# Four pairs of conditioning units move from layer 0's FFN to the norm in the middle of layer 1

## The reference

```python
def adaln(c, w, b):
    return jnp.split(jax.nn.silu(c) @ w + b, 6, axis=-1)

def modulate(x, g, shift, scale):
    return rms_norm(x, g) * (1.0 + scale[:, None, :]) + shift[:, None, :]

for layer in range(DEPTH):
    mp = adaln(c_prompt, w_ada[layer], b_ada[layer])
    ms = adaln(c_sample, w_ada[layer], b_ada[layer])
    hp = modulate(yp, g_mix[layer], mp[0], mp[1])
    hs = modulate(ys, g_mix[layer], ms[0], ms[1])
    ...  # mixer: convolution and linear attention in layer 0, gating and window attention in layer 1
    yp = yp + mp[2][:, None, :] * (op @ w_out[layer])
    yp = swiglu_sublayer(yp, mp[3], mp[4], mp[5], g_ffn[layer], w_ffn_gate[layer],
                         w_ffn_up[layer], w_ffn_down[layer])
    ...  # the same for ys
```

## Time and profile before

| what | value |
|---|---|
| median of 3 runs | 2774.05 us (2773.72 to 2775.11) |
| the profiled execution | 2771.56 us, span 2769.8 us |
| PE busy | 2686.3 us, 97% of the span |
| DVE, ACT, POOL busy | 1427.0, 1161.6, 96.4 us |
| granted TensorE clock, mean | 0.986 |
| DMA | 603.61 MB, 218 GB/s over the span |

### The profile page before, as it was taken

One profiled execution on the slowest core, in us unless ns is written; L12 is line 12 of the kernel. 1 busy time (PEld: TensorE's weight loads), 2 busy tenths in 40 slices (PEclk: granted clock), 3 DMA queues, 4 the chain that ended last, 5 costly groups with the idle time before them and its releaser, 6 DMA issues.

```text
span 2769.8 us, 48514 instructions
## 1 busy us (share of the span) xinstructions
PE 2686.3 (97%) x20155; PEld 2479.4 (90%) x20155; DVE 1427.0 (52%) x1983; ACT 1161.6 (42%) x1521; POOL 96.4 (3%) x136
## 2 busy tenths in 40 slices
PE   5899999999999999999999999998999999999998
PEld 1688987889889888998999899898999999999998
DVE  0588957564444333444544556656554444444444
ACT  2433255454343322343443446535444433444433
POOL 1100011110000000000000000001000000000000
PEclk7999999999999999999999999999999999999999
DMA  9877769677777788777465454334545455455453
GB/s 399 360 288 273 289 234 167 266 273 277 284 272 283 273 315 329 281 277 264 154 233 163 143 184 138 101 124 164 165 165 167 140 167 181 164 167 167 137 164 127
DMA packets 110043, 603.61 MB, mean 218 GB/s; under 512 B 24830, under 2 KB 26302, under 8 KB 53579
## 3 DMA queue, kind: packets, MB, share of 16 engines
q1 hardware_dynamic: 109898, 601.56, 62.2%
HBM read 592.02 MB, written 9.49 MB: 217 GB/s over the span
## 4 chain that ended last, share of the span: by engine, by line
PE 89%; DMA 5%; DVE 3%; ACT 2%; issue 1%; SPq 0%; DVEq 0%; ACTq 0%
PE ps L880 26%; PE ps L882 25%; PE ps L881 25%; PE ps L1086 5%; DMA pre_ring<-in_w_ada 2%; DMA aring<-in_w_ada 1%; ACT w_hi L1400 1%; PE ps L1068 1%; PE ps L1099 1%; DMA raw<-in_w_dn 1%; DVE w_lo L1870 1%; PE ps L1236 0%; PE ps L1054 0%; DMA raw<-in_w_out 0%; PE ps L1055 0%
## 5 line engine op out<-in xcount | busy, mean ns | idle before, releaser
L1870 DVE TENSOR_TENSOR w_lo<-raw,w_hi 128x2048 fp32r<-128x2048 f32 (+2 forms) x410 | 804.1, 1962 | 1033.3 <-ACT w_hi L1400 1033.2
L880 PE MATMUL ps<-act_hi,w_hi 128*128 128x288 f32 x4128 | 1234.7, 299 | 11.0 <-DVE w_lo L1870 9.0
L881 PE MATMUL ps<-act_hi,w_lo 128*128 128x288 f32 x4128 | 1220.1, 296 | 0.0
L882 PE MATMUL ps<-act_lo,w_hi 128*128 128x288 f32 x4128 | 1215.9, 295 | 0.0
L1400 ACT ACTIVATE w_hi<-raw 128x2048 fp32r<-128x2048 f32 (+2 forms) x410 | 674.3, 1645 | 1056.4 <-PE ps L882 1033.0
L880 PEld LDWEIGHTS ps<-act_hi,w_hi 128*128 128x128 f32 x4128 | 776.1, 188 | 63.8 <-issue 59.9
L882 PEld LDWEIGHTS ps<-act_lo,w_hi 128*128 128x128 f32 x4128 | 779.3, 189 | 0.0
L881 PEld LDWEIGHTS ps<-act_hi,w_lo 128*128 128x128 f32 x4128 | 777.4, 188 | 0.0
L880 PE MATMUL ps<-hid_hi,w_hi 128*128 128x288 f32 x1408 | 418.8, 297 | 0.6 <-DVE w_lo L1870 0.6
L881 PE MATMUL ps<-hid_hi,w_lo 128*128 128x288 f32 x1408 | 415.4, 295 | 0.0
L882 PE MATMUL ps<-hid_lo,w_hi 128*128 128x288 f32 x1408 | 414.0, 294 | 0.0
(11 more groups left out here) (329 smaller groups left out, 1772.7 us busy)
## 6 DMA issues: line engine op xcount, KB each, us to landing
raw<-in_w_gu SPq DMA_DIRECT2D x172, 1024.0 KB, 5.3
aring<-in_w_ada SPq DMA_DIRECT2D x166, 1024.0 KB, 6.9
raw<-in_w_dn SPq DMA_DIRECT2D x128, 704.0 KB, 4.1
raw<-in_w_ab SPq DMA_DIRECT2D x40, 1024.0 KB, 6.5
raw<-in_w_out SPq DMA_DIRECT2D x64, 512.0 KB, 4.4
raw<-in_w_cd SPq DMA_DIRECT2D x26, 1024.0 KB, 5.3
pre_ring<-in_w_ada SPq DMA_DIRECT2D x16, 1024.0 KB, 9.4
side<-in_w_ada SPq DMA_DIRECT2D x6, 1024.0 KB, 10.9
```

The lines of the kernel that those rows point to most:

```text
L880: pe.matmul(bank, w_hi[:, h, cols], hi[:, kt, :], start=begin, stop=False)
L881: pe.matmul(bank, w_lo[:, h, cols], hi[:, kt, :], start=False, stop=False)
L882: mm = pe.matmul(bank, w_hi[:, h, cols], lo[:, kt, :], start=False, stop=end)
L1870: dve.tensor_tensor(w_lo[:, h, 0:w], raw[:, par, h * KT * P:h * KT * P + w], w_hi[:, h, 0:w].bitcast(F32), ALU.subtract).then_inc(split_do ...
```

## The change

Pairs 73 to 76 leave layer 0's FFN. Its second `gu` group now has 9 pairs, 64 to 72. Norm 2 keeps three pairs, now 73, 74 and 75, with the turn of double 18 behind them instead of double 19's. Norm 3 gets four, 76 to 79, and double 19's turn behind its first step. Pair 76 lies in `free_hi` and `free_lo`, 77 and 78 in `side`, 79 in `aring`; SP loads all four in the third step of `OUT1B`, the last ones after the stores of layer 1's mixer outputs.

Pairs in norm 3 need `cond`, whose place `wsp` has taken by then. So DVE copies `cond` to `cond_kept` in the `kv` step. That is a part of `mods` whose rows belong to layer 0 and are not read any more. SP waits for that copy (`cond_log` 2) before it loads the constants of `q`. In the second step of `OUT1B` DVE clears `cond`'s padding and copies the vectors back.

```diff
--- before.py
+++ after.py
@@ -45,9 +45,9 @@
 MIX_PAIRS = 20
-UNDER_NORM = {1: (24, 25), 2: (77, 78, 79)}
+UNDER_NORM = {1: (24, 25), 2: (73, 74, 75), 3: (76, 77, 78, 79)}
 HELD = MIX_PAIRS
-SIDE_PAIRS = HELD, 24, 25, 77, 78
+SIDE_PAIRS = HELD, 24, 25, 73, 74, 76, 77, 78
@@ -103,7 +103,7 @@
         else:
-            segs += [Seg("gu", 0, 7, 2, 22, 64, range(1, 14)), Seg("gu", 0, 4, 2, 36)]
+            segs += [Seg("gu", 0, 7, 2, 22, 64, range(1, 10)), Seg("gu", 0, 4, 2, 36)]
@@ -294,6 +294,7 @@
             g_high = sb("g_high", [P, 512], stack=a)
+            cond_kept = sb("cond_kept", [P, KT, S9], stack=a)
@@ -394,7 +395,7 @@
         ada_landed = [sem("ada_landed0"), sem("ada_landed1")]
-        side_landed = {k: sem(f"side_landed{k}") for k in UNDER_NORM}
+        side_landed = {k: sem(f"side_landed{k}") for k in (1, 2)}
@@ -473,8 +474,8 @@
             n = 4 * ADA_N
-            if p == HELD or p in UNDER_NORM[1]:
-                return side[:, 0 if p == UNDER_NORM[1][1] else 1, r]
+            if p == HELD or p in UNDER_NORM[1] + UNDER_NORM[3][1:3]:
+                return side[:, 0 if p in (UNDER_NORM[1][1], UNDER_NORM[3][2]) else 1, r]
@@ -482,15 +483,20 @@
-            return 1 if p == HELD else next(k for k in UNDER_NORM if p in UNDER_NORM[k])
+            return 1 if p <= UNDER_NORM[1][1] else 2
...
-            return {HELD: 32, 24: 96, 25: 96}.get(p, 64)
+            return {HELD: 32, 24: 96, 25: 96, 73: 64, 74: 64}.get(p, 160)
...
             return UNDER_NORM.get(RESTARTS.index(seg.n0) + 1, ()) if seg.n0 in RESTARTS else ()
+
+        def last_double(seg, ls):
+
+            pairs = norm_pairs(seg)
+            return pairs[-1] // 4 if ls == 0 and pairs and pairs[-1] % 4 == 3 else None
@@ -661,8 +667,16 @@
                             load_pair(UNDER_NORM[2][2])
-                    if seg is OUT1B and i is None and base == 0 and j == 1:
+                    if seg is OUT1B and ls == 1:
                         store_values()
+                    if seg is OUT1B and ls == 2:
+                        sp.wait_ge(half_done, 2 * seg.n0)
+                        load_pair(UNDER_NORM[3][0])
+                        load_pair(UNDER_NORM[3][3])
+                        sp.wait_ge(sguv_stored, 16)
+                        sp.wait_ge(cache_stored, 16 * 6)
+                        for p in UNDER_NORM[3][1:3]:
+                            load_pair(p)
@@ -768,7 +782,8 @@
                         sp.wait_ge(rows_set, 1)
-                        sp.wait_ge(ada_used, 4 * PRE + 2 * PAIRS)
+                        sp.wait_ge(ada_used, 4 * PRE + 2 * UNDER_NORM[3][0])
+                        sp.wait_ge(cond_log, 2)
@@ -975,7 +990,7 @@
                 pe.wait_ge(drained, Q_SEG.n0)
-                pe.wait_ge(ada_biased, PRE + PAIRS // 4)
+                pe.wait_ge(ada_biased, PRE + PAIRS // 4 - 1)
@@ -1142,13 +1157,15 @@
                     if first and n in RESTARTS:
+                        if seg.kind == "gu" and seg.layer:
+                            pe.wait_ge(cond_ready, 2)
...
                         restart(n, par)
-                        if seg.kind == "kv" and norm_pairs(seg):
-                            double_turn(PAIRS // 4 - 1)
+                        if last_double(seg, ls) is not None:
+                            double_turn(last_double(seg, ls))
@@ -1586,8 +1603,8 @@
                         double_copy(pair_of(seg, ls) // 4)
-                    if seg.kind == "kv":
-                        double_copy(PAIRS // 4 - 1)
+                    if i is None and base == 0 and last_double(seg, ls) is not None:
+                        double_copy(last_double(seg, ls))
@@ -1654,6 +1671,8 @@
                     act.wait_ge(ada_used, 4 * PRE + 2 * UNDER_NORM[2][g // 2] + 2)
+                if k == 3 and g == 2:
+                    act.wait_ge(ada_used, 4 * PRE + 2 * UNDER_NORM[3][0] + 2)
@@ -2041,7 +2060,7 @@
                     if seg.by_halves and seg.norm_next and end:
-                        dve.wait_ge(ada_biased, PRE + (4 if seg.norm_next == 1 else 20))
+                        dve.wait_ge(ada_biased, PRE + (4 if seg.norm_next == 1 else 19))
@@ -2056,7 +2075,7 @@
                         if end and seg.norm_next:
-                            dve.wait_ge(ada_biased, PRE + {1: 4, 2: 19}.get(seg.norm_next, 20))
+                            dve.wait_ge(ada_biased, PRE + {1: 4, 2: 18}.get(seg.norm_next, 20))
@@ -2105,8 +2124,15 @@
                         double_bias(pair_of(seg, ls) // 4)
+                    if i is None and base == 0 and last_double(seg, ls) is not None:
+                        double_bias(last_double(seg, ls))
                     if seg.kind == "kv":
-                        double_bias(PAIRS // 4 - 1)
+                        dve.tensor_copy(cond_kept[:], cond[:, :, 0:S9]).then_inc(cond_log, 1)
+                    if seg is OUT1B and ls == 1:
+                        dve.wait_ge(cond_log, 2)
+                        dve.wait_ge(wr_ready, 1)
+                        dve.memset(cond[:, :, S9:32], 0.0)
+                        dve.tensor_copy(cond[:, :, 0:S9], cond_kept[:]).then_inc(cond_ready, 1)
@@ -2494,7 +2520,7 @@
                 if seg == "norm":
-                    dve.wait_ge(ada_biased, PRE + {1: 6, 2: 19}.get(norms, 20))
+                    dve.wait_ge(ada_biased, PRE + {1: 6, 2: 18, 3: 19}.get(norms, 20))
```

## The result

The changed kernel takes 2786.78 us (median of 5 runs, 2785.44 to 2790.23) against 2774.05 us for the kernel before in the same session (5 runs, 2772.85 to 2777.2). The ratio is 1.005, with a 95% interval of 1.004 to 1.0061. The profiled execution took 2785.44 us; its span is 2783.7 us, 13.9 us more than before.

A forecast was written before the change was run, and what follows sets the result against it. PE was taken as the bound, busy 97% of the span, so costs count when PE waits. -9.1 + 7.2 + 11.2 + 2 x 2.0 + 1.2 = +14.5 us on the 2774.05 us median gave 2788.5 us; range 2779 to 2792 us.

The forecast's parts named there:

- The likeliest case: The forecast itself, with a new PE stall in q and one in OUT1B: 2788.5 us, chance 78%.
- Step 1: Layer 0's FFN: four pairs and double 18's turn leave, all of it counting on PE, -9.1 us.
- Step 2: q's second step: SP waits for the kept copy, starts 8.8 us later, and 7.2 us reach PE.
- Step 3: OUT1B's fifth step: weights land behind eight 1 MB loads on SP's queue, PE loses 11.2 us (9.9 at 421 GB/s).
- Step 4: After each of the two new waits PE runs at half clock for a while: 2.0 us more each.
- Step 5: Norm in the middle of layer 1: four pairs fill PE's idle time, double 19's turn follows, +1.2 us.
- upper sum: Sum with 11.5 us for the burst, 2.7 us per wait and clock lost at the turn: +18.2 us.
- (a): SP's queue serves loads side by side, so small loads pass the burst: 2768.2 us, faster by 0.2%, chance 5%.
- (b): Only the burst's stall in OUT1B is absent: +1.3 us, 2775.4 us, no change, chance 6%.
- (c): Only the stall in q from SP's wait for the copy is absent: +5.3 us, 2779.3 us, chance 6%.

The follow-up runs named there:

- both: Changed kernel with cond copied in layer 0's down projection and norm 3's four pairs loaded singly over four OUT1B steps: 2766.6 us, ratio 0.9982.
- early copy: Changed kernel, but DVE copies cond to cond_kept in layer 0's down projection instead of the kv step: 2779.3 us, ratio 1.0023 to the kernel before.
- Spread: Changed kernel, but norm 3's four pairs are loaded one by one in OUT1B steps 2, 3, 5 and 6: 2775.59 us, ratio 1.0009.
- the kernel with POOL's queue: Changed kernel, but POOL issues the same eight 1 MB loads on its own queue instead of SP: 2777.81 us, ratio 1.0012.

## Why the prediction was right, step by step

I predicted 2788.5 us, 14.5 above the kernel before; it is 2786.78, 12.7 above (13.9 by the profiles). The likeliest case came, with the two stalls and the path to each as told. Its parts can be priced one by one. Some come closer to the forecast than their working deserves.

- **Step 1, pairs leave the FFN, -9.1.** The two profiles differ by 8.0 us. PE's short waits in that stretch (0.3 us and more) sum to 3.4 us before and 4.6 after, at places that change from run to run; without them it is 9.2. The kernel with both repairs has 3.2 us of them and gains 9.4. The steps without pairs lie 12.80 us apart, as the earlier trace rows said: ACT's timeline after has

```profile
1310.16 0.39 ACT L1463 ACTIVATE sg<-ps 128x288 f32<-128x288 f32 x1
1322.96 0.39 ACT L1463 ACTIVATE sg<-ps 128x288 f32<-128x288 f32 x1
```

- **Step 2, SP waits for the copy, +7.2.** SP started 28.25 - 19.69 = 8.6 us later (8.8 predicted), and PE waited 7.28 us. The early copy took just this away. That the wait agrees to 0.1 us is luck, as two things that I hadn't foreseen cancel. The landing doesn't shift as far as the issue: counted from the sums of norm 2, ACT began on the weights at 1593.81 - 1558.63 = 35.18 us before and at 1594.67 - 1552.00 = 42.67 us now, 7.5 us later and not 8.6. And PE came to the step 1.3 us sooner than before, as this profile lacks a stretch at the lower clock. "Spread" and the kernel with POOL's queue wait for the same copy and have that stretch: there PE waited 5.47 and 6.00 us.
- **Step 3, the burst, +11.2.** PE waited 10.82 us, between my two values of 11.2 (0.397 MB per us) and 9.9 (421 GB/s). The load behind the burst landed at 1859.9 + 20.5 = 1880.4; the burst had begun at 1854.79, so 8.39 MB and 0.52 MB took 25.6 us less 2.4, which is 0.384 MB per us. The stall stands where predicted, in the fifth step: it begins at 1882.86 - 10.82 = 1872.04, with four steps still to run, the stalled one counted.
- **Step 4, the clock, 2 x 2.0.** Like for like the second stall costs 3.3 us of clock, where I assumed 2.0. Behind the wait the level is low until about 1886.5. But it falls once more, 20 us later, while PE works without a gap (length, PE busy, clock, DMA share, GB/s):

```profile
1907.00:1911.00 4.00, 4.00 (x21) 0.57 0.88 297
```

"Early copy" has this second fall too, and "both" hasn't; by the granted clock a fall of this length costs 1.7 us. Whether the stall brings it isn't shown. The q stretch grew by 9.5 with a wait of 7.3: 2.2 us. Together 5.5 instead of 4.0. Steps 2 and 4 together are 9.7 us for the copy and 13.6 for the burst by the profiles that differ in nothing else ("spread" and "early copy" against "both"), where I had 7.2 + 2.0 = 9.2 and 11.2 + 2.0 = 13.2. The profile of after lacks three short stretches at the lower level that before has (end of this text), 1.5 us each, so that its rows in the table seem to show less: 1.5 us less ahead of q, and 11.1 instead of 13.6 us in the out projection.
- **Step 5, norm 3, +1.2.** From the sums to the next step it was 1925.24 - 1902.14 = 23.10 us before and is 1939.05 - 1914.62 = 24.43 now, +1.3. The pairs end at 1922.08 + 1.90 = 1923.98, behind the restart stands the wait of 1.05 us for `adarow`, and the granted clock is 1.00 where the earlier trace rows had 0.50.
- **The start**, of which I said nothing, is 1.4 us longer in this profile. It lies between 589.3 and 594.2 us in the eight kernels' profiles, though none of them changes it.
- **The range.** Its upper sum was added up wrongly: -9.1 + 7.2 + 11.5 + 2 x 2.7 + 1.2 + 1.5 is +17.7, not +18.2. The end of 2792 us stays as it is.

Of the rivals, (a) "side by side" is rejected by the 20.5 us to landing. Between two queues a small load did get past much of the burst (9.1 us), within one it did not. (b) and (c), in which one stall is absent, are each what an experiment built by undoing that stall: 2775.59 us against 2775.4 for (b), and 2779.3 against 2779.3 for (c). That both agree to 0.2 us is luck, with single runs 10 us apart: against the kernel before of their own session they are 2.4 and 6.2 us slower, where (b) said 1.3 and (c) 5.3. But the prices hold within some 1 us.

## What to carry to other kernels

A load is late by what stands ahead of it on its own queue: ask of each burst how many bytes it puts ahead of the next load that is wanted, and compare that time with the cover (here some 9 to 10 us, from two slots of `raw`). Spreading the same bytes over the steps left the out projection 0.3 us longer than before (126.70 against 126.38 us), although the DMA engines were full. And when a place in memory is given to a new use earlier, do the copy that frees it as early as its data allow, not where it happens to be needed, since a queue behind it waits.

## What the runs showed that I had not expected

**Short stretches at the lower clock come and go with the run.** Before, PE has one of 3 to 4 us near 1584 in kv and q's first step, and two in `OUT1`, each while it works without a gap. The kernel after has none of the three; "early copy", "spread" and "both" have all of them, at the same places in the program. By stretch (length, PE busy, clock, DMA share, GB/s), 20 us and 50 us after the beginning of `OUT1`, first the kernel after and then "early copy":

```profile
1797.00:1805.00 8.00, 7.83 (x52) 1.00 0.42 132
1827.00:1835.00 8.00, 7.85 (x52) 1.00 0.41 133
```

```profile
1789.00:1797.00 8.00, 7.84 (x41) 0.79 0.42 131
1819.00:1827.00 8.00, 7.85 (x41) 0.79 0.41 131
```

Each costs some 1.5 us (in norm 2's stretch 39.33 against 37.83 us). When the constants are loaded doesn't decide it: "spread" loads them as late as the kernel after and has the stretch in kv all the same. So in the profiles the early copy gains less than the stall of q was worth, and a part of the 1.8 us by which its median missed my number may be this; medians can't tell it. What sets the stretches off stays open: no run here was made to tell.

**A queue of its own gave no more than a good order in one queue.** The second queue halved the delay of the small load next to the burst, but stretched the burst and the loads after it, to 17.5 us for 512 KB, and a wait of 4.35 us came two steps behind the place of the old one. In the traces that is 3.4 us worse than the spread loads, in the medians it doesn't show.
